# Homes of their own for the first sixteen weight units, and the S5 tables spread over the first dense tiles

## What is computed

```python
c_act = jax.nn.silu(c)
ada = c_act @ w_ada[l] + b_ada[l]                    # 1024 -> 6144
sh_m, sc_m, g_m, sh_f, sc_f, g_f = jnp.split(ada, 6, axis=-1)
h = modulate(rms_norm(x), sh_m, sc_m)                # norm(x) * (1 + sc_m) + sh_m
proj = h @ w_in[l]                                   # 1024 -> 2304
z, u = proj[..., :D_SHIFT], proj[..., D_SHIFT:]      # 14 and 4 tiles of 128 columns
z = z + mu_shift[l] * (z_prev - z)                   # then RWKV-7 on z, S5 on u
...
dt = jnp.exp(log_dt)[:, None]                        # S5: tables from parameters alone
abar = exp(dt * a);  coef = (abar - 1) / a
bbar_re = coef_re[..., None] * b_re - coef_im[..., None] * b_im
...
x = x + g_m[:, None, :] * mix                        # then the FFN, then two more layers
```

## Time and profile before

| | |
|---|---|
| median of 3 runs | 1703.81 us (1702.84 to 1709.72) |
| profiled execution, its own time | 1708.99 us |
| span of the profiled execution | 1707.2 us |
| PE busy | 1517.9 us (89%) |
| DVE busy | 813.6 us (48%) |
| ACT busy | 581.1 us (34%) |
| POOL busy | 269.6 us (16%) |
| moved by DMA | 144.17 MB, mean 84 GB/s |

### The profile page before, as it was taken

The page is one execution under the profiler, slowest core; times in us unless marked ns, Lnnn a source line. Parts: engine busy times, 40 slices in busy tenths (PEclk is TensorE's granted clock), DMA queues, the critical chain, the costliest instruction groups (busy, mean ns, idle before and its releaser), DMA issues.

```text
span 1707.2 us, 23771 instructions
## 1 busy us (share of the span) xinstructions
PE 1517.9 (89%) x10024; PEld 1176.7 (69%) x10024; DVE 813.6 (48%) x1291; ACT 581.1 (34%) x1002; POOL 269.6 (16%) x224
## 2 busy tenths in 40 slices
PE   4799876887789999999989899988898999998889
PEld 1477765775468888888866687756686677766667
DVE  8554637713554333232345545446534455445642
...
GB/s 245 160 63 51 100 133 125 55 177 134 37 74 87 99 94 92 99 130 87 99 88 50 38 75 62 62 50 37 62 99 93 37 61 55 71 69 30 50 86 62
DMA packets 51849, 144.17 MB, mean 84 GB/s; under 512 B 13216, under 2 KB 17952, under 8 KB 50976
## 3 DMA queue, kind: packets, MB, share of 16 engines
...
...
## 4 chain that ended last, share of the span: by engine, by line
PE 67%; DVE 14%; ACT 9%; issue 4%; DMA 2%; POOL 2%; SPq 1%; DVEq 0%; ACTq 0%
PE b L383 66%; ACT arena L2093 5%; DVE arena L1234 4%; DVE ring L1234 2%; DVE arena L1242 2%; DVE X L1234 1%; ACT ring L2096 1%; PE b L386 1%; ACT L2093 1%; DVE arena L1923 1%; POOL arena L2727 1%; DMA ring<-in_ws 1%; DMA scr_kpad<-arena 1%; ACT arena L2096 1%; DMA arena<-scr_yd 1%
## 5 line engine op out<-in xcount | busy, mean ns | idle before, releaser
L383 PE MATMUL b<-tile,ring 128*128 128x512 f32 x2288 | 707.7, 404 | 20.0 <-POOL tile L2724 9.3
L383 PE MATMUL b<-HR,ring 128*128 128x512 f32 (+1 forms) x1888 | 623.3, 406 | 62.8 <-DVE ring L1234 28.0
L383 PEld LDWEIGHTS b<-tile,ring 128*128 128x128 f32 x2288 | 439.8, 193 | 127.5 <-issue 19.6
L383 PEld LDWEIGHTS b<-HR,ring 128*128 128x128 f32 (+1 forms) x1888 | 363.5, 193 | 164.1 <-issue 59.9
L1234 DVE TENSOR_TENSOR ring<-ring,ring 128x1024 fp32r<-128x1024 f32 x186 | 255.8, 1377 | 316.3 <-ACT ring L2096 315.4
L383 PE MATMUL b<-arena 64*64 64x64 f32 (+10 forms) x3072 | 237.8, 288 | 48.2 <-issue 26.1
L2096 ACT ACTIVATE ring<-ring 128x1024 fp32r<-128x1024 f32 x186 | 195.9, 1054 | 215.3 <-PE b L383 212.3
L383 PEld LDWEIGHTS b<-arena 64*64 64x64 f32 (+5 forms) x3072 | 153.2, 149 | 121.9 <-issue 83.1
L2096 ACT ACTIVATE arena<-b 128x512 f32<-128x512 f32 (+3 forms) x136 | 74.2, 570 | 279.5 <-PE b L383 232.2
L1234 DVE TENSOR_TENSOR arena<-arena 128x512 f32<-128x512 f32 (+7 forms) x194 | 100.3, 549 | 71.1 <-ACT arena L2093 49.1
L2724 POOL TENSOR_TENSOR tile<-arena,tile 128x512 fp32r<-128x512 f32 x38 | 50.7, 1340 | 467.8 <-ACT tile L2096 467.8
(11 more groups left out here) (108 smaller groups left out, 1030.1 us busy)
## 6 DMA issues: line engine op xcount, KB each, us to landing
ring<-in_ws SPq DMA_DIRECT2D x234, 512.0 KB, 3.5
...
```

Of the source, the lines that this page charges most:

```text
L383: return self.e.matmul(out, lhsT, rhs, start=start, stop=stop, skip_group_check=True)
```

## The change

Sixteen units, those of both ada groups, come first in the order of weights and have places of their own (`homes`: fifteen parts of the arena and rows 6 and 7 of H) and semaphores of their own (e0 to e15, `landed`). SP issues in one go units 0 to 7, the dense units 16, 17 and 18, units 8 to 15, and unit 19, and behind these twenty the write of kpad's padding; the reloads of `whole_done` for the first sixteen are gone. PE does group 1's units after row 2 in place of after row 3. DVE does 14 of the steps at the start in place of 20 (the ten short ones and four of the sixteen), one after each row of the first tiles (eight), and the last four after the evictions of the six tiles. ACT's wait for the end of the tables is gone (DVE waits instead, once). The load of w2 and one pair of POOL's memsets wait for the ada units whose homes they use. Line numbers in the changed file are 8 to 11 higher in the parts that the rows name.

```diff
--- before.py
+++ after.py
@@ -15,6 +15,7 @@
 NT = 8
 DFF_T = 22
 RING = 4
+EARLY = 16
 UNITS = 234
 SBUF = 229344
 FIRST = [12, 13, 4, 5, 0, 8]
@@ -211,12 +212,17 @@
         return [self.ring2[:, b * 2048 + i * 1024:b * 2048 + i * 1024 + 1024] for i in (0, 1)]

     def wraw(self, u):
-        return self.ring[:, u % RING * 1024:u % RING * 1024 + 1024]
+        return self.homes[u] if u < EARLY else self.ring[:, u % RING * 1024:u % RING * 1024 + 1024]
+
+    def landed(self, u):
+        return self.s(f"e{u}" if u < EARLY else f"w{u % RING}", 16)

     def views(self):
         R = self.region
         self.cact32 = self.nst[:, 8:264].rearrange("p (r c) -> p r c", c=32)
         self.one_sc = self.nst[:, 536:544]
+        self.homes = [*(R(4 * i, 1024) for i in range(7)), R(88, 1024), *(R(52 + 4 * i, 1024) for i in range(7)),
+                      self.H[:, 6:8, :].rearrange("p a t -> p (a t)")]
         self.omm, self.omk = self.nst[:, 544:558], self.nst[:, 560:564]
         self.GC = self.nst[:, 572:604].rearrange("p (n c) -> p n c", n=4)
         self.r_, self.r2_, self.re_ = self.nst[:, 0:4], self.nst[:, 4:8], self.nst[:, 608:612]
@@ -354,8 +360,9 @@
                 return
             yield

-    def dense_tiles(self, n, parts, rows=8):
-
+    def dense_tiles(self, n, parts, rows=8, also=()):
+
+        also = iter(also)
         self.ahead()
         next(parts)
         next(parts)
@@ -363,6 +370,7 @@
             if r < rows - 2:
                 next(parts)
             self.blocks(n)
+            next(also, None)

     def play(self, order, **parts):
         for c in order:
@@ -448,11 +456,13 @@
         k = self.k
         tiles = [("in", n) for n in FIRST]
         ready = self.split_h("h1", True)
+        k.order += [("ada", n, r) for g in (0, 1) for r in range(8) for n in ADA[g]]
         self.norm_first()
         self.ada_units(0, range(8))
         self.ada_sum(0)
-        self.dense_rows(tiles, ready, rows=range(4))
+        self.dense_rows(tiles, ready, rows=range(3))
         self.ada_units(1, range(8))
+        self.dense_rows(tiles, ready, rows=range(3, 4))
         self.ada_sum(1)
         self.dense_rows(tiles, ready, rows=range(4, 8))
         for n in FIRST:
@@ -488,13 +498,14 @@

         k = self.k
         for r in rows:
-            u = len(k.order) // 8
-            k.order += [("ada", n, r) for n in ADA[g]]
+            u = 8 * g + r if g < 2 else len(k.order) // 8
+            if g >= 2:
+                k.order += [("ada", n, r) for n in ADA[g]]
             if r == 0:
                 for h in (0, 1):
                     self.take(("col", g, h))
             self.wait_ge(k.s("c_act"), "c")
-            self.wait_ge(k.s(f"w{u % RING}", 16), u)
+            self.wait_ge(k.landed(u), u)
             q = 32 * (r % 4)
             for h in (0, 1):
                 ins = self.mm(k.bank["col", g, h][q:q + 32, :], k.cact32[:, r, :], k.wraw(u)[:, h * 512:h * 512 + 512],
@@ -1261,19 +1272,19 @@
         D = k.s("dense")
         self.wait_ge(k.s("in0", 16), "par")
         tables = self.s5_tables()
-        for _ in range(20):
+        for _ in range(14):
             next(tables)
         parts = self.first_parts()
-        self.units(8)
-        self.dense_tiles(6, parts, 4)
-        for _ in tables:
-            pass
-        self.units(8)
-        self.dense_tiles(6, parts, 4)
+        self.units(EARLY)
+        self.dense_tiles(6, parts, 4, tables)
+        self.dense_tiles(6, parts, 4, tables)
         self.ts(k.omm, k.pc("mu", 0, 14), -1.0, ALU.mult, 1.0, ALU.add).then_inc(*k.s("z_omm").inc(0))
         self.ts(k.omk, k.pc("k_a", 0, 4), -1.0, ALU.mult, 1.0, ALU.add).then_inc(*k.s("prep_dve").inc("omk"))
         for n in FIRST:
             self.shifted(n)
+        for _ in tables:
+            pass
+        self.wait_ge(k.s("tab"), SOFAR)
         self.play(PREP, z=self.in_proj(), p=self.prep())
         self.play(MIX, r=self.rwkv(), s=self.s5_apply(), a=self.ada_columns(), g=self.group_norm(), o=self.begin_outs())
         x1 = k.s("x1")
@@ -2349,8 +2359,6 @@
                 if half:
                     self.wait_ge(pe, ("rk", n - 2))
                     self.wait_ge(dve, ("kg", n - 2))
-                else:
-                    self.wait_ge(k.s("tab"), "end")
                 self.af(y, k.KK[n], ACT.Square, scale=k.pc("k_k", n)).then_inc(*act.inc(("kk", n)))
             for n, (sg, as_, cs, gam, ig, y, q) in W:
                 self.wait_ge(pe, ("sg", n))
@@ -2732,11 +2740,12 @@
     def program(self):
         k = self.k
         self.e.memset(k.nst[:, 8:264], 0.0).then_inc(*k.s("ones_pool").inc("c"))
-        for n in (0, 1):
-            self.e.memset(k.prep(n)[3][:, :, 0], 1.0).then_inc(*k.s("ones_pool").inc(n))
         self.e.memset(k.zero, 0.0).then_inc(*k.s("mat_pool").inc("zero"))
         for j in range(2):
             self.e.memset(k.TMP[:, j, 0:1], 0.0).then_inc(*k.s("z_pad").inc(j))
+        self.wait_ge(k.s("ada_pe"), ("cols", 1))
+        for n in (0, 1):
+            self.e.memset(k.prep(n)[3][:, :, 0], 1.0).then_inc(*k.s("ones_pool").inc(n))
         self.play(MIX, r=self.rwkv(), s=self.s5_apply())
         for n in range(DFF_T):
             self.wait_ge(k.s("ffn_act"), ("hi", n))
@@ -2914,7 +2923,7 @@

     def load(self, u):
         k = self.k
-        self.e.dma_start(k.wraw(u), k.d["ws"][u, :, :]).then_inc(*k.s(f"w{u % RING}", 16).inc(u))
+        self.e.dma_start(k.wraw(u), k.d["ws"][u, :, :]).then_inc(*k.landed(u).inc(u))

     def unit(self, u):

@@ -2924,7 +2933,7 @@

     def whole_done(self, u):

-        if u + RING < UNITS:
+        if EARLY <= u < UNITS - RING:
             self.wait_ge(self.k.s("ada_pe"), ("unit", u))
             self.load(u + RING)

@@ -2935,19 +2944,17 @@
         for i in range(2):
             self.e.dma_start(k.X[:, 4 * i:4 * i + 4, :], d["xT"][:, 4 * i:4 * i + 4, :]).then_inc(*k.s(f"x_{i}", 16).inc(0))
         self.e.dma_start(k.cst[:, :], d["cst"]).then_inc(*k.s("cst", 16).inc(0))
-        self.load(0)
-        self.load(1)
         self.e.dma_start(k.s5p, d["s5p"]).then_inc(*k.s("s5w", 16).inc(0))
-        self.load(2)
-        self.load(3)
+        for u in (*range(8), *range(EARLY, EARLY + 3), *range(8, EARLY), EARLY + 3):
+            self.load(u)
         self.wait_ge(k.s("mat_pool"), "zero")
         self.e.dma_start(d["kpad"].rearrange("g c n -> c g n")[:, :, 0:112], k.zero).then_inc(*k.s("kpad", 16).inc("zero"))
-        self.units(8)
+        self.units(EARLY)
         self.ahead()
         for r in range(4):
             self.blocks(6)
+        self.wait_ge(k.s("ada_pe"), ("cols", 0))
         self.e.dma_start(k.w2, d["small"][:, 0, :]).then_inc(*k.s("small", 16).inc(0))
-        self.units(8)
         self.ahead()
         for r in range(4):
             self.blocks(6)
```

## The result

| | before | changed |
|---|---|---|
| median, runs side by side on one chip | 1704.56 us (20 runs) | 1710.9 us (20 runs) |
| ratio, 95% interval | | 1.0034 [1.0023, 1.0046] |
| span of the profiled execution | 1707.2 us | 1711.0 us |
| PE busy | 1517.9 us | 1512.7 us |
| PE idle before its dense matmuls (the page's `b<-HR,ring` group), all / before splits by DVE | 62.8 / 28.0 us | 84.4 / 36.4 us |

The change makes the kernel slower by 0.34%, 5.8 us of 1704.56 by the ratio. The prediction was 1709.6 us, 5.8 us above the median it started from.

What follows compares the result with a forecast made beforehand. It took DVE, started by a DMA, to bound the start, and four ring slots with their DMAs the stretch to row 4; +7.6 - 11.1 + 7.6 + 1.7 = +5.8 us on 1703.81 gave 1709.6 us, range 1700 to 1718.

Steps and rivals of the forecast that it cites:

- Term 1: The start: the padding lands later, at about 38.7 us, and DVE's row 0 moves from 41.86 to 49.5, +7.6 us.
- the padding's landing is the queue's end: At the start: the padding's write lands when SP's load queue runs dry, so sixteen more units delay it by 20.2 us.
- rival 2: At the start: the long load queue runs slower, at 300 GB/s, moving everything by 7.8 us more, to 1717.4; chance 0.14.
- Term 2: From DVE's row 0 to PE's row 4: ada units without DMA waits, 29.8 us against 40.88, -11.1 us.
- Term 3: After the six tiles: DVE's table steps delay the split of unit 23, so tile 9 starts +7.6 us later.
- Term 4: PE's clock: the new 6.9 us idle ahead of tile 9 brings a restart at 0.50, +1.7 us.
- the clock at row 4 would stay low: At PE's row 4: less idle gives back none of the 1.6 us lost to the 0.50 clock; taken as zero.
- From tile 9 on, all by about 5.8 later: From tile 9 to the kernel's end: everything keeps its distances, shifted by about 5.8 us.
- Rival 1: At the start: the padding's write overtakes the loads and lands at 18.5 us, making the kernel 1689.4 us; chance 0.08.
- Rival 3: The stall before tile 9 is absorbed by PE's later waits, Term 3 and Term 4 vanish, 1700.3 us; chance 0.12.

Runs made afterwards that it cites:

- e7: The changed kernel with the padding's write behind eleven of the twenty unit loads and ahead of the other nine; 1697.50 us, ratio 0.9961.
- e1: The changed kernel with the padding's write ahead of all twenty unit loads; 1690.23 us against 1706.01, ratio 0.9905.
- e6: The changed kernel's homes alone, with the table steps placed as in the kernel before; 1721.38 us against 1703.83, ratio 1.0102.
- e2: The changed kernel with the last four table steps moved off the split of unit 23, two of them among rows 0 to 3; 1703.46 us, ratio 0.9987.
- e8: The changed kernel with seven extra unused f32 matmuls on PE ahead of tile 9; 1708.51 us against 1704.98, ratio 1.0033.

## Why the prediction was right, point by point

**Term 1 (+7.6, measured +7.93).** The padding was to land at about 38.7 and the first long step to start with it; it started at 39.17, after 21.09 us of idle ended by `scr_kpad`. The rate was 416 GB/s from the earlier trace rows; the windows of the changed kernel show 401 to 422 between 10 and 36 us, and e7 gives 403 over nine loads. The step that carried it, "the padding's landing is the queue's end", is shown by e1 and e7. One thing in it was not as told: I wrote of a long queue with twenty-six DMAs in it. SP could not issue them at its usual pace: after the first few an issue took 1 us and more, one 3.10, so that the padding was issued only at 23.02. That changed nothing, since the queue was never dry: it moved 401 GB/s or more in the windows up to 36 us. Two small readings were off and cost nothing: `ada_sum(0)` ended at 28.3, not by 27, and by the prediction's own numbers rival 2 decides below about 367 GB/s, not 363.

**Term 2 (-11.1, measured -11.30).** 29.58 us against the 29.8 of the sum. The ada units have no DMA in the way (66.30), ACT splits unit 20 at 74.44 and PE starts 4.93 us later, the number taken from before. The four steps stayed under PE's rows. What steps cost that don't, e6 shows: with its last six in one run ahead of the splits the stretch takes 35.77 us.

**Term 3 (+7.6, measured +7.58).** From row 4 to tile 9 34.59 us, where the count gave 34.6. It was a count down DVE's list by durations from the earlier trace rows. e2 removed the stall by the order of that list alone.

**Term 4 (+1.7, measured +1.26 at tile 9).** The clock fell to 0.50 and cost 1.3 us, as e8 shows on its own. That it was so near the estimate is in part luck: the same stall of 6.95 us costs 2.9 us in e7. That the clock at row 4 would stay low was right too: 0.50 between 80 and 82 us. It is not one price, though: in e6 the clock stayed at 0.50 for 6.1 us after a restart, and cost 1.5 us more than in the kernel before.

**What was off.** "From tile 9 on, all by about 5.8 later" holds to 200 us (5.48) and not behind it, in the one pair of executions: about 3 at 386 us. The median of twenty runs shows 5.8, and part of so good a match is luck: the interval is 3.9 to 7.8. What shortens the distance by some 2 us in the trace, between 200 and 390 us, is open.

**The rivals.** Rival 1 did not come true, and its price was about right (e1: -16.2 us by the ratio, -13.0 at z9, for -14.4). Rival 2 needed less than some 367 GB/s; it was 401 to 422. Rival 3 falls for the stage that it spoke of: the stall of 6.95 us is there and stays as a shift. What the runs add is how near the better kernel was: the forecast held the gain of some 20 us that lay in the place of one DMA, as a rival with the chance 0.08, and priced it, but as something that might happen by itself.
